# A decoder layer with sixteen experts: the first expert's start reordered, and the next expert's spare product moved forward

## What is computed

```
proj = x @ w_in                       # split: short conv, stick-breaking attention, gated linear attention
mix  = concat(y_conv, y_sb, y_gla) @ w_out
x    = layer_norm(ALPHA * x + mix)
scores = sigmoid(x @ router_w)        # 16 experts in 4 groups
# the best group (sum of its two best), in it the 2 best experts; weights normalised to sum 1
for e in range(16):
    h = silu(x @ w1[e]) * (x @ w3[e])         # 1024 -> 512
    y = y + gate[:, e] * (h @ w2[e])          # 512 -> 1024
out = layer_norm(ALPHA * x + y)
```

## Time and profile before

| | |
|---|---|
| median of three runs | 982.16 us (976.93 to 989.33) |
| profiled execution | 973.72 us, span 972.1 us |
| TensorE busy | 920.5 us, 95% |
| VectorE, ScalarE, GpSimd busy | 612.2, 483.8, 198.3 us |
| TensorE in the chain of waits | 86% |
| HBM traffic | 173 GB/s over the span |

### The profile page before, as it was taken

The page is one execution under the profiler, slowest core; times in us unless marked ns, Lnnn a source line. Parts: engine busy times, 40 slices in busy tenths (PEclk is TensorE's granted clock), DMA queues, the critical chain, the costliest instruction groups (busy, mean ns, idle before and its releaser), DMA issues.

```text
span 972.1 us, 19175 instructions
## 1 busy us (share of the span) xinstructions
PE 920.5 (95%) x7435; PEld 747.1 (77%) x7435; DVE 612.2 (63%) x815; ACT 483.8 (50%) x779; POOL 198.3 (20%) x242
## 2 busy tenths in 40 slices
PE   8999999999999999979999889999999999999980
PEld 6778998996777777768887578888888888888860
DVE  4211833665665755686665797777777777777786
ACT  3222532225564654561222266666666666666674
POOL 3000000000000000041000185433333334344144
PEclk9999999999999999999999799999999999999995
DMA  9301111001100031049532289999999999999974
GB/s 260 70 22 43 45 49 39 1 2 44 44 22 23 23 77 44 1 148 375 200 119 92 96 186 313 357 326 321 315 322 315 323 317 321 316 315 319 320 254 169
DMA packets 102670, 168.84 MB, mean 174 GB/s; under 512 B 25532, under 2 KB 49212, under 8 KB 102608
## 3 DMA queue, kind: packets, MB, share of 16 engines
q1 hardware_dynamic: 88720, 143.74, 44.1%
q0 software_dynamic: 10848, 23.09, 9.4%
q10 hardware_dynamic: 3040, 1.19, 0.6%
HBM read 143.76 MB, written 24.54 MB: 173 GB/s over the span
## 4 chain that ended last, share of the span: by engine, by line
PE 86%; DVE 7%; ACT 3%; DMA 2%; issue 1%; POOL 0%; SPq 0%; POOLq 0%; DVEq 0%; ACTq 0%
PE bank L863 14%; PE bank L865 14%; PE bank L864 14%; PE pz L863 7%; PE pz L864 7%; PE pz L865 7%; PE pz L1210 5%; PE pz L1234 3%; PE pz L979 3%; PE bank L1057 2%; PE bank L1073 2%; PE bank L1199 1%; DVE el L1939 1%; DMA x_row<-in_x_dram 1%; DMA sum_scratch<-yA,tab 1%
## 5 line engine op out<-in xcount | busy, mean ns | idle before, releaser
L1939 DVE TENSOR_TENSOR el<-er,eh 128x1024 fp32r<-128x1024 f32 x192 | 225.7, 1224 | 50.6 <-ACT eh L1543 48.5
L1543 ACT ACTIVATE eh<-er 128x1024 fp32r<-128x1024 f32 x192 | 190.4, 1053 | 8.6 <-PE pz L865 8.6
L1871 DVE TENSOR_TENSOR_SCAN Qs<-Qs,own 128x128 f32<-128x128 f32 (+7 forms) x48 | 65.0, 1355 | 69.7 <-ACT Qs L1430 69.7
L863 PE MATMUL bank<-xT_hi,w_hi 128*128 128x512 f32 (+1 forms) x264 | 106.3, 403 | 1.9 <-DVE xT_lo L1756 1.9
L865 PE MATMUL bank<-xT_hi,w_lo 128*128 128x512 f32 (+1 forms) x264 | 102.4, 388 | 0.0
L864 PE MATMUL bank<-xT_lo,w_hi 128*128 128x512 f32 (+1 forms) x264 | 101.7, 385 | 0.0
L863 PE MATMUL pz<-eh,xh 128*128 128x512 f32 x256 | 101.6, 397 | 0.0
L864 PE MATMUL pz<-el,xh 128*128 128x512 f32 x256 | 99.8, 390 | 0.0
L865 PE MATMUL pz<-eh,xl 128*128 128x512 f32 x256 | 99.7, 390 | 0.0
L627 POOL MEMSET rw<- 128x128 f32 x1 | 0.2, 207 | 415.2 <-DVE mix L1864 415.2
L863 PE MATMUL bank<-w_hi,xT_hi 128*128 128x384 f32 x192 | 65.0, 338 | 1.3 <-ACT kteN L1445 1.3
(11 more groups left out here) (335 smaller groups left out, 1810.5 us busy)
## 6 DMA issues: line engine op xcount, KB each, us to landing
er<-in_w_dram SPq DMA_DIRECT2D x192, 512.0 KB, 9.7
w_raw<-in_w_in_dram SPq DMA_DIRECT2D x21, 512.0 KB, 3.9
x_row<-in_x_dram SPq DMA_DIRECT2D x8, 512.0 KB, 8.9
xres<-in_x_dram SPq DMA_DIRECT2D x8, 512.0 KB, 5.6
x_scratch<-x SPq DMA_DIRECT2D x8, 512.0 KB, 2.6
sum_scratch<-x SPq DMA_DIRECT2D x8, 512.0 KB, 3.9
cx<-sum_scratch SPq DMA_DIRECT2D x8, 512.0 KB, 8.2
out_dram<-cx SPq DMA_DIRECT2D x5, 512.0 KB, 2.9
```

What stands on the lines that cost most here:

```text
L863: pe.matmul(dst, lh, rh, start=(k == k_first), stop=False)
L1543: act.activation(eh[:, p, :], er[:, p, :], ACT.Copy).then_inc(S["eh_ok"], 1)
L1871: dve.tensor_tensor_scan(Qs[:, h, 0:W][:, ::-1], Qs[:, h, 0:W][:, ::-1], own1[:, T - W:][:, ::-1], 0.0, ALU.mult, ALU.max).then_inc(S["sca ...
L1939: dve.tensor_tensor(el[:, p, :], er[:, p, :], eh[:, p, :].bitcast(F32), ALU.subtract).then_inc(S["el_ok"], 1)
```

## The change

It has two parts.

**Expert 0.** GpSimd gathers the quarters of expert 0 ahead of its rows, on a semaphore of their own (xgB_in). TensorE's slots order is 0 first, with fillers and gates, then slot list 1 with its gates; 6 fillers stand where there were 8 + 6. Then it transposes the quarters, does the w1 half of spare_gu, transposes the rows, does the w3 half. It waits for the slot factors only ahead of spare_y. VectorE makes the split of the gates ahead of the second slot list, subtracts pieces 1 and 2 between the routing steps, finds the pass of each row by rounding (three steps) in place of a chain of six comparisons, and makes the slot factors of experts 0 to 2 together in expert 0. The second list of rows (`second_rows`) moves behind x_lo, and pieces 10 and 11 behind hA and hTl. ScalarE rounds all pieces of expert 0 ahead of the transposes.

**Experts 1 to 13.** Behind `spare_y(b)` stands `spare_gu(b + 1)`, ahead of the rows by w2. For this the quarters of b + 1 are transposed ahead of hA, and ScalarE converts all three parts of x ahead of hTh. Expert 14 keeps the old order for expert 15 and is written out; the loop runs 3 to 13. Two semaphores of the end are joined into one to make room for xgB_in.

```diff
-            with eng.Fori(3, NE - 1) as e:
+            with eng.Fori(3, NE - 2 if one else NE - 1) as e:
...
-                for buf, src, ids in ((xgAs[b % 2], x1_dram, firstA), (xgBs[b % 2], x1_quarters, firstB)):
+                for buf, src, ids, done in ((xgBs[b % 2], x1_quarters, firstB, "xg_in" if b else "xgB_in"), (xgAs[b % 2], x1_dram, firstA, "xg_in")):
...
-            for b in range(2):
-                slot_tokens(b)
-            spin(8)
-            for b in range(2):
-                slot_gates(b)
+            slot_tokens(0)
             spin(6)
+            slot_gates(0)
+            slot_tokens(1)
+            slot_gates(1)
...
             def spare_y(b):
-                if not first_block(b):
+                if first_block(b):
+                    pe.wait_ge(S["slotF_ok"], 4)
+                    pe.wait_ge(S["padadd_ok"], 4)
+                else:
                     pe.wait_ge(S["yB_ev"], b)
...
             def pe_block(b, nxt, buf=0, nbuf=0):
-                pe.wait_ge(S["xTh_ok"], NXR * b + (1 if first_block(b) else NXR))
-                spare_gu(b)
+                if first_block(b):
+                    pe.wait_ge(S["xTh_ok"], 1)
+                    spare_gu(b, 0)
+                    x_transposes(b, (0, 1), buf)
+                    spare_gu(b, 1)
+                elif isinstance(b, int) and not ahead(b - 1):
+                    pe.wait_ge(S["xTh_ok"], NXR * b + NXR)
+                    spare_gu(b)
...
                 pe.wait_ge(S["hA_ok"], b + 1)
+                if nxt and ahead(b):
+                    x_transposes(b + 1, (2,), nbuf)
...
                 spare_y(b)
+                if nxt and ahead(b):
+                    pe.wait_ge(S["xTh_ok"], NXR * (b + 1) + NXR)
+                    spare_gu(b + 1)
...
             def act_block(b, nxt, buf=0, nbuf=0):
-                piece_hi(b, 4)
-                piece_hi(b, 5)
+                if not first_block(b):
+                    piece_hi(b, 4)
+                    piece_hi(b, 5)
...
                 if nxt:
-                    x_hi(b + 1, (0,))
+                    x_hi(b + 1, ROUNDS if ahead(b) else (0,))
...
-            link(dve.tensor_scalar(rtmp[:, :, :], rpos[:, 0:NT, :], float(TW), None, ALU.is_ge))
-            for j in range(2, MAXPASS):
-                link(dve.scalar_tensor_tensor(rtmp[:, :, :], rpos[:, 0:NT, :], float(j * TW), rtmp[:, :, :], ALU.is_ge, ALU.add))
-            for b in range(2):
-                slot_factors(b)
+            link(dve.tensor_scalar(rtmp[:, :, :], rpos[:, 0:NT, :], -0.5 * (TW - 1), 1.0 / TW, ALU.add, ALU.mult))
+            link(dve.tensor_scalar(rtmp[:, :, :], rtmp[:, :, :], WHOLE, None, ALU.add))
+            link(dve.tensor_scalar(rtmp[:, :, :], rtmp[:, :, :], -WHOLE, None, ALU.add))
...
             def dve_block(b, nxt, buf=0, nbuf=0):
-                for p in range(6, NPIECE):
-                    piece_lo(b, p)
+                piece_lo(b, 6)
+                piece_lo(b, 7)
                 if first_block(b):
                     slot_rows(2)
-                    slot_factors(2)
+                    for c in range(3):
+                        slot_factors(c)
+                last = NPIECE - 2 if first_block(b) else NPIECE
+                for p in range(8, last):
+                    piece_lo(b, p)
...
                 dve.tensor_tensor(hA[:, :], silA[:, :], uA, ALU.mult).then_inc(S["hA_ok"], 1)
+                if first_block(b):
+                    piece_lo(b, NPIECE - 2)
```

More of the change, by code:

```diff
@@ L125 @@
 BIG = float(1 << 20)
+WHOLE = 1.5 * 2.0 ** 23
 LAST = NE - 1
@@ L432, in experts_of @@
             block(NE * j + 2, True)
-            with eng.Fori(3, NE - 1) as e:
+            one = isinstance(j, int)
+            with eng.Fori(3, NE - 2 if one else NE - 1) as e:
                 block(NE * j + e, True)
-            if isinstance(j, int):
-                last(NE * j + NE - 1)
+            if one:
+                block(NE - 2, True)
+                last(NE - 1)
             else:
@@ L475, in first_block, with next_to_last, ahead @@
             return isinstance(b, int) and b == 0
+        def next_to_last(b):
+            return isinstance(b, int) and b == NE - 2
+        def ahead(b):
+            return not first_block(b) and not next_to_last(b)
         def norm_stats(dve, buf, s, src, n, done, i, read):
@@ L1182, in slot_gates @@
                 last.then_inc(S["sidg_ps"], 1)
[L1184 to L1188 removed]
+            slot_tokens(0)
             spin(6)
+            slot_gates(0)
+            slot_tokens(1)
+            slot_gates(1)
             def x_transposes(b, rounds, buf=0):
                 xgA, xgB = xgAs[buf], xgBs[buf]
[L1195 removed]
+                if first_block(b) and rounds == (2,):
+                    pe.wait_ge(S["xgB_in"], 16)
+                else:
+                    pe.wait_ge(S["xg_in"], 32 * b + 16)
                 for r in rounds:
@@ L1200, in x_transposes, with spare_gu @@
                     last.then_inc(S["xtr_ps"], 1)
-            def spare_gu(b):
-                for p in range(2 * NF):
+            def spare_gu(b, m=None):
+                for p in range(2 * NF) if m is None else range(NF * m, NF * m + NF):
                     pe.wait_ge(S[f"e_in{p}"], 16 * b + 16)
@@ L1288, in pe_block @@
                 last.then_inc(S["hTA_ps"], 1)
-                if nxt:
+                if nxt and not ahead(b):
                     x_transposes(b + 1, (2,), nbuf)
                 spare_y(b)
+                if nxt and ahead(b):
+                    pe.wait_ge(S["xTh_ok"], NXR * (b + 1) + NXR)
+                    spare_gu(b + 1)
                 pe.wait_ge(S["hTl_ok"], b + 1)
@@ L1580, in _ @@
             exps(NT - 1, NT)
-            piece_hi(0, 2)
-            piece_hi(0, 3)
+            for p in range(2, NPIECE):
+                piece_hi(0, p)
             def x_hi(b, rounds, order=ROUNDS):
@@ L1609, in act_block @@
                 if nxt:
-                    x_hi(b + 1, (1, 2))
+                    if not ahead(b):
+                        x_hi(b + 1, (1, 2))
                     piece_hi(b + 1, 0)
@@ L2212, in dve_pass @@
                 if isinstance(j, int):
-                    for p in range(1, AHEAD):
+                    for p in range(3, AHEAD):
                         piece_lo(b0, p)
                     slot_hits(2)
+                    second_rows()
                 experts_of(dve, j, dve_block, dve_last)
```

70 lines of the change are left out of this document (41 added, 29 removed).

## The result

The kernel after takes 1000.5 us (median of four runs, 997.5 to 1005.5) beside 979.5 us of the kernel before (median of four, 976.7 to 989.3): ratio 1.021, 95% interval 1.016 to 1.026. It is slower, by about 2%; the prediction was 976 us and "within 2%". The profiled execution took 998.69 us, span 997.0.

What follows compares the result with a forecast made beforehand. TensorE, busy 95% of the span, was taken as the bound (VectorE in expert 0). The terms -2.7 - 2.6 + 1.0 = -4.3 us gave 977.9 from the median, 975.2 from the middle of all four; forecast 976 us, range 966 to 986.

Steps and rivals of the forecast that it cites:

- part 1: Experts 1 to 13: next expert's first spare product moves behind this one's second; gain 2.6 us, bounds 0 and 2.9.
- part 2: Expert 0: reordered gathers, transposes, spare_gu and VectorE work; gain 2.7 us, bounds 1.8 and 4.1.
- covered: Expert 0's second gather lands by 554 us and is wanted later, so its delay was taken to cost nothing.
- steady gain per expert: Experts 1 to 13: two changes of matmul shape go, 0.22 us per expert, less 0.02 for VectorE.
- expert 2's weights, once: Expert 2's last weight load lands at 605.5 us, wanted at 604.3; cost 1.0 us once, bounds 0 and 3.
- expert 0: hA of expert 0 ends at 574.5 us instead of 577.18; gain 2.7 us, bounds 1.8 and 4.1.
- The forecast of 0.06 for this: Experts 1 to 13: VectorE loses its 1.5 us to spare ahead of hA, delaying it 0.06 us at most.
- 10.88: Experts 1 to 13: us from the rows' second product's last matmul start to the next first product's last matmul.
- rival (b): TensorE's clock stays at 2.4 GHz through the routing for spare_gu; expert 0 gains 4.1 us, total 974.6; chance 0.10.
- Rival (a): VectorE takes the steady gain: a hand-over adds 0.2 us, pitch stays 23.93 us, total 978.6; chance 0.22.
- Rival (c): Weights late in every expert at the moved spare_gu: 986 us at 11.8 us landings, 1025 at 14.8; chance 0.10.
- sum: Whole kernel: gains of 2.7 and 2.6 us less a cost of 1.0, 4.3 us faster, bounds -7.0 and +1.2.

Runs made afterwards that it cites:

- c_held: Whole change, with GpSimd's indirect transfers held until the moved spare products (expert 0: spare_gu) are done, on chip C; 0.996 of the kernel before.
- steady_held: Steady half alone (expert 0 as before), with the gather and addition behind it held until the moved spare product is done, chip B; 0.994 of before.
- c_after: The kernel after, unchanged, run on chip C beside its halves; 1.022 of the kernel before.
- c_steady: Steady half alone (new order in experts 1 to 13, expert 0 as before), on chip C; 996.0 us, 1.013 of the kernel before.
- after_again: The kernel after, unchanged, run once more on chip B beside the kernel before; span 994.6 us.
- before_two: The kernel before, unchanged, run for its trace on chip B; span 976.2 us.
- steady_only: New order in experts 1 to 13 alone, expert 0 as in the kernel before, on chip A; 973.7 us where before made 972.6.
- one_inc: Kernel after with two semaphore increments (raw_done by 4) per spare product instead of eight, on chip D; 969.3 us, 0.997 of before.
- all_apart: Whole change with GpSimd's indirect DMAs kept out of every spare product, expert 2's gather between the two scatter sets, chip E; 976.0 us, 0.997.
- interleaved: Kernel after with one eighth of the moved spare product behind each group of three matmuls of rows_y, chip D; 28 us slower than before.
- expert0_only: Changed expert 0 alone, all other experts as in the kernel before, on chip A; 969.3 us where before made 972.6.
- pool_held: Kernel after with GpSimd's indirect transfers held by a wait on raw_done until the moved spare products (expert 0: spare_gu) are done; time not given.
- expert0_held: Changed expert 0 alone, with its second gather and the scatters held until spare_gu(0) is done, on chip D; 1.006 of before.
- c_expert0: Changed expert 0 alone, all other experts as in the kernel before, on chip C; time not given.

## Why the prediction was wrong

**The step that failed** is "No matmul is added or removed" in part 1, and in part 2 the 1.8 to 3.6 us for the second half of spare_gu: both took it that a matmul costs the same wherever it stands. Where the result was measured, and on chips B and C, the 128 small matmuls cost 0.8 to 2.3 us more in their new place, beside GpSimd's gather and addition (1.5 in the mean of the kernel after's 13), and the second half of spare_gu(0), beside eight scatters, took 12.6 us where it takes 1.9 without stalls. The prediction moved the gathers and scatters 1.9 us forward and asked when their data was wanted ("covered"); it never asked what stood on TensorE while they were issued. Shown by `c_held` and `steady_held` against `c_after` and `c_steady`: holding these DMAs back takes the stalls away, 1.022 to 0.996 on chip C, and 1.013 (chip C) to 0.994 (chip B, so not one comparison) for the steady half.

The loss by the traces of one chip (`after_again` less `before_two`, spans 994.6 and 976.2): expert 0, hA at 583.56 against 578.03, +5.5; expert 1 -1.9 (before has its own stall there); experts 2 to 14, from hA(1) to hA(14), 326.7 against 311.8, +14.9. Together hA(14) comes 18.6 us later, and the span is 18.4 us longer.

**The sign that was there**: the profiled execution lay 8.4 us under the median of the runs, and the prediction set that aside as an offset of the level. `before_two` shows what was missing in it: stalls of 3.9 and 2.1 us in the spare products of experts 0 and 1. The kernel before takes 972.6 to 973.0 us on A and D, and 978.4 to 981.2 on B, C and E. Durations were read from a trace without the stalls, for runs of which at least the kernel after's has them; of the kernel before's timed runs (976.7 to 989.3) it is likely by their times and not shown.

**Without stalls the forecast steps held, read in the traces**:

| step | forecast | measured |
|---|---|---|
| steady gain per expert | 0.20 (0 to 0.22) | 0.29 (23.93 to 23.64, `steady_only`) |
| expert 2's weights, once | 1.0 (0 to 3) | 2.0 in `steady_only` (hA(1) to hA(2) 25.6 against the new pitch of 23.64), 5.6 in `one_inc`, whose raw_done comes later, nothing in `all_apart` |
| expert 0 | 2.7 (1.8 to 4.1) | 2.8 |
| sum | 4.3 | 3.7 in time (`one_inc`); on chip A 3.3 for expert 0's half and a loss of 1.1 for the steady half |

The kernel after itself never ran on a chip without stalls. The steady half alone is 1.001 of before there (0.999 to 1.003), though its trace gains 1.9 us from hA(1) to hA(14) (309.3 against 311.1 in the trace of before); its gain in time is not shown.

The steady gain is larger than forecast because a step was left out: the one from the last small matmul to the large one behind it, 0.20 us (708.88 less 705.25 and 3.43) where a small step is 0.027. With it TensorE gains some 0.37 us, as `interleaved` has it (0.35). VectorE takes 0.07 of that back: hA now comes 0.51 us behind the rows' last matmul, without a pause ahead of it, where it came 0.43 behind. The forecast of 0.06 for this was right; two small slips, 10.88 for 10.90 in TensorE's pace and 1.0 for the 1.2 us that 605.5 less 604.3 makes, change nothing.

For expert 0 the two traces of chip A are set against their last common step, VectorE's copy of rpos, since one reached it 2.5 us earlier; `steady_only`, which has the old expert 0, then `expert0_only`:

```profile
543.28 0.31 DVE L2005 COPY rpos<-bank 128x144 f32<-128x144 f32 x1
```

```profile
540.82 0.31 DVE L2013 COPY rpos<-bank 128x144 f32<-128x144 f32 x1
...
555.58 1.43 DVE L1974 TENSOR_TENSOR xl<-bank,xh 128x512 fp32r<-128x512 f32 x2 [1.44 <-ACT xh L1615]
```

hA follows 32.95 us behind it in the old order (576.23) and 30.12 in the new (570.94). VectorE waits 1.44 us for x, as forecast (1.4), because the clock did fall; PEclk, third number from the end, is 0.50 from 550 to 554 us:

```profile
550.00:552.00 2.00, 1.77 (x36) 1.65 (x40) 1.76 (x8) 0.18 (x1) 0.00 (x0) 0.50 0.32 125
```

TensorE's waits in 540 to 550 us were of 0.97 us at most. So rival (b) is out, and the trace disagrees with the rule that it came from (the Trainium skill, "TensorE: Matmul & The Clock Gate", section "Why this matters for your kernels"), which would have given 4.1. Rival (a) is out: hA came 11.39 us behind the rows' product and the pitch fell by more than forecast. Rival (c) had the right sign and the wrong mechanism: a landing of 14.8 us in every expert. In `steady_only` TensorE waited on the moved product's pieces in expert 2 alone; the stalls are not on loads, since `c_held` needs the same pieces at the same place without them, and since `slot_gates`, which needs none, has them too. No rival had "GpSimd's DMAs beside the moved product", though the timeline of POOL would have given its place.

**Left open.** What in the chip holds the matmuls. The runs show the place (small matmuls, float32 and bf16, beside an indirect DMA's issue and transfer; now and then also a large one of the rows: 0.8 and 1.0 us in `c_steady`, 0.5 in `c_after`, 0.4 in `before_two`), not whether it is the writing of descriptors or the transfer, and not why some chips do it and others don't. That it is the chip rests on every kernel traced there: four on A and four on D without the stalls, four on B, four on C and two on E with them, one trace of each. The chips of the very first two traces are not on record. Whether the stall needs dense small matmuls was to be told by `interleaved`, which ran only on chip D. The Trainium skill, "DMA: Bandwidth & Descriptors", section "Latency and other measured facts", guesses that the fetching of descriptors from GpSimd's rings crowds the ports that DMA engines 7 and 15 use; it says nothing of TensorE there, and no run here shows it.

## What to carry to other kernels

Before moving work on TensorE, read what the other engines issue in the microseconds of its new place, GpSimd's gathers, scatters and additions above all; and when you move those, read what TensorE does beside them. A wait on an event that is there anyway (here raw_done) keeps the two apart, and took the whole change from 1.022 to 0.996 on chip C; what queues behind the wait has to be looked at too (7.1 us in `pool_held`, 5.0 in `expert0_held`). When the one profiled execution is under nearly all timed runs, ask what the others have that it lacks before you subtract from it.

## What the runs showed of the hardware

- The same program runs differently on chips that look alike: the kernel before takes 972.6 and 973.0 us on two chips and 978.4 to 981.2 on three; the steady half alone 973.7 and 996.0. TensorE's small matmuls (128*32, 128 columns) beside an indirect DMA of GpSimd advance by a few every 0.7 to 1.4 us on the one kind (expert 0, beside the scatters) and at 27 ns each on the other. GpSimd's issue itself is no slower: the first eight scatters take 10.0 us in `c_expert0` and 12.2 in `expert0_only`, the same program.
- While TensorE is held, other engines learn of its finished work late: the first four transposes of expert 0's rows start at 556.79 us in the kernel after and should be done by 557.8, but their semaphore update is noted at 567.73, and ScalarE, which waits for nothing else, starts at 567.75. In `expert0_only` the update comes at 554.93, with the fourth transpose's end at 554.92.
- Going from 128*128 to 16 matmuls of 128*32 and back costs 0.35 us beyond the matmuls: eight such visits per expert made the kernel 28 us slower.
- GpSimd's DRAIN at the program's end takes 7.4 and 7.1 us in the two traces of chip E and 1.2 to 1.3 in the other eighteen.
